# Seven block products in place of eight for 20 of the 22 column blocks of the first feed-forward matrix

## The reference, cut to what matters

```
def swiglu(x, w_in, w_out):
    a, b = jnp.split(x @ w_in, 2, axis=-1)
    return (jax.nn.silu(a) * b) @ w_out
...
        h = swiglu(x, w_ffn_in[l], w_ffn_out[l])
        x = layer_norm(ALPHA * x + h, ln3_g[l], ln3_b[l])
```

## Time and profile before

| | |
|---|---|
| median of 3 runs | 891.89 us (891.59 to 893.75) |
| the profiled execution's own time | 891.73 us |
| its span (first to last instruction) | 890.0 us |
| TensorE busy | 879.4 us, 99% |
| weight loads busy | 732.5 us, 82% |
| VectorE busy | 420.9 us, 47% |
| ScalarE busy | 292.3 us, 33% |
| GpSimd busy | 53.2 us, 6% |

### The profile page before, as it was taken

One profiled execution on the slowest core, in us unless ns is written; L12 is line 12 of the kernel. 1 busy time (PEld: TensorE's weight loads), 2 busy tenths in 40 slices (PEclk: granted clock), 3 DMA queues, 4 the chain that ended last, 5 costly groups with the idle time before them and its releaser, 6 DMA issues.

```text
span 890.0 us, 11559 instructions
## 1 busy us (share of the span) xinstructions
PE 879.4 (99%) x4519; PEld 732.5 (82%) x4519; DVE 420.9 (47%) x780; ACT 292.3 (33%) x544; POOL 53.2 (6%) x85
## 2 busy tenths in 40 slices
PE   8999999999999999999999999999999999999996
PEld 8988898877678888888889788888888888888885
DVE  4344357778533434434767693333333333322344
ACT  4112167238632222222325552222222222111221
POOL 3100000262300000000000010000000000000000
PEclk9999999999999999999999999999999999999999
DMA  8535532330013232326605111222222224323211
GB/s 283 161 95 141 119 96 60 107 95 2 1 49 94 95 95 94 94 94 236 220 18 189 48 49 48 94 94 94 94 94 94 94 94 142 105 102 105 104 81 71
DMA packets 70502, 90.11 MB, mean 101 GB/s; under 512 B 2861, under 2 KB 62071, under 8 KB 70463
## 3 DMA queue, kind: packets, MB, share of 16 engines
q1 hardware_dynamic: 70079, 89.15, 30.9%
q0 software_dynamic: 384, 0.43, 0.3%
HBM read 87.05 MB, written 2.52 MB: 101 GB/s over the span
## 4 chain that ended last, share of the span: by engine, by line
PE 96%; issue 1%; DVE 1%; DMA 1%; ACT 0%; SPq 0%; DVEq 0%; POOLq 0%; POOL 0%
PE ps L1738 28%; PE ps L1739 28%; PE ps L1740 28%; PE ps L1903 3%; PE ps L1980 2%; PE ps L1940 2%; PE ps L1775 1%; DMA x_nat<-in_x 1%; PE ps L2322 1%; PE ps L2323 1%; PE ps L2324 1%; PE ps L2252 0%; PE ps L1949 0%; PE ps L2255 0%; PE ps L2253 0%
## 5 line engine op out<-in xcount | busy, mean ns | idle before, releaser
L1738 PE MATMUL ps<-xt_hi,w_hi 128*128 128x512 f32 (+1 forms) x688 | 267.6, 389 | 0.2 <-DVE w_lo L1694 0.2
L1739 PE MATMUL ps<-xt_hi,w_lo 128*128 128x512 f32 (+1 forms) x688 | 266.8, 388 | 0.0
L1740 PE MATMUL ps<-xt_lo,w_hi 128*128 128x512 f32 (+1 forms) x688 | 266.8, 388 | 0.0
L1738 PEld LDWEIGHTS ps<-xt_hi,w_hi 128*128 128x128 f32 x688 | 129.2, 188 | 27.4 <-issue 0.6
L1740 PEld LDWEIGHTS ps<-xt_lo,w_hi 128*128 128x128 f32 x688 | 129.2, 188 | 26.4
L1739 PEld LDWEIGHTS ps<-xt_hi,w_lo 128*128 128x128 f32 x688 | 129.2, 188 | 26.3
L895 ACT CAST w_hi<-raw 128x1024 fp32r<-128x1024 f32 (+1 forms) x58 | 60.0, 1037 | 180.4 <-PE ps L1740 172.0
L1178 DVE TENSOR_TENSOR w_lo<-raw,w_hi 128x1024 fp32r<-128x1024 f32 (+1 forms) x58 | 70.1, 1210 | 91.1 <-ACT w_hi L895 90.7
L1694 DVE TENSOR_TENSOR w_lo<-raw,w_hi 128x1024 fp32r<-128x1024 f32 x40 | 48.9, 1222 | 79.1 <-ACT w_hi L1137 79.1
L1487 DVE TENSOR_TENSOR w_lo<-raw,w_hi 128x1024 fp32r<-128x1024 f32 x30 | 36.7, 1223 | 90.1 <-ACT w_hi L1062 90.1
L1137 ACT CAST w_hi<-raw 128x1024 fp32r<-128x1024 f32 x40 | 41.9, 1047 | 78.8 <-PE ps L1740 78.8
(11 more groups left out here) (288 smaller groups left out, 1293.8 us busy)
## 6 DMA issues: line engine op xcount, KB each, us to landing
raw<-in_w_in SPq DMA_DIRECT2D x24, 1024.0 KB, 5.0
raw<-in_w_ffn_in SPq DMA_DIRECT2D x22, 1024.0 KB, 4.9
raw<-in_w_ffn_out SPq DMA_DIRECT2D x11, 1024.0 KB, 4.8
raw<-in_w_mix_out SPq DMA_DIRECT2D x4, 1024.0 KB, 4.8
raw<-in_w_branch_b SPq DMA_DIRECT2D x4, 512.0 KB, 4.0
resid<-in_x SPq DMA_DIRECT2D x1, 2048.0 KB, 9.5
raw<-in_w_xkv SPq DMA_DIRECT2D x2, 1024.0 KB, 5.7
raw<-in_w_in SPq DMA_DIRECT2D x3, 512.0 KB, 4.1
```

The costliest lines, as they stand in the source:

```text
L1738: pe.matmul(dst, a_hi, b_hi, start=start, stop=False)
L1739: pe.matmul(dst, a_lo, b_hi, start=False, stop=False)
L1740: return pe.matmul(dst, a_hi, b_lo, start=False, stop=stop)
```

## The change

The first group of four pieces stays. The remaining 20 double pieces of 256 columns ("blocks", n = 0 to 19; even ones are of the silu half, odd ones of the other half, and a pair of them gives two slices of hidden activations) are each computed by Winograd's form of Strassen's scheme. Each block is seen as a product of 2 by 2 quarters: the 1024 summed columns in two halves, the 256 weight columns in two halves of 128, the 512 rows in two halves of 256. Seven products of quarters, P1 to P7, take the place of eight. Each product is 4 slices by 3 matmuls of 128 weight columns against 256 rows, 12 matmuls; a block is 84 matmuls of 256 rows where it was 48 of 512.

Four sums of quarters of the activations are made once (`SUM1` to `SUM4`; GpSimd makes two inputs and SUM3, VectorE the rest), and split like everything else (`sum_round` on ScalarE, `sum_rest` on VectorE). Four sums of quarters of the weights are made by VectorE for each block: `t1`, `t2`, `t3` (in place in `raw`) and `t4`. Each of the seven weight operands is split by ScalarE (`op_round`) and VectorE (`op_rest`) into one of four slots of half the old size. Three bank copies per block by ScalarE (`seed`, `hold_u2`, `hold_u3`) and two additions by VectorE (`add_c22`, `add_c12`) bring the products together. ScalarE instead of VectorE now rounds the hidden activations (`round_first`, `round_second`). SyncE loads each block as two halves of 512 KB; the loops are written out. In the first slice of the second matrix TensorE takes the four tiles of 128 rows in the order 0, 2, 1, 3 in place of 2, 3, 0, 1.

In the diff `pool` is GpSimd, `act` ScalarE, `dve` VectorE and `pe` TensorE; the first `ffn_block` is ScalarE's, the second VectorE's, and the loop after it VectorE's too. GpSimd calls `left_sums` ahead of the last norm's first `rstd`.

```
+def products_in_order():
+    order = []
+    for n in range(N_BLOCK):
+        order.append(("P1", n))
+        if n:
+            order.append(("P4", n - 1))
+        order.append(("P5", n))
+        if n:
+            order.append(("P3", n - 1))
+        order += [("P6", n), ("P2", n), ("P7", n)]
+    return order + [("P4", N_BLOCK - 1), ("P3", N_BLOCK - 1)]
...
+            def left_sums():
+                pool.wait_ge(turn_lo, 4 * TT + 4)
+                pool.tensor_tensor(F11, xt_hi[:, 0:4, LO].bitcast(F32), xt_lo[:, 0:4, LO].bitcast(F32), ALU.add).then_inc(left_sum, 1)
+                pool.tensor_tensor(F12, xt_hi[:, 4:8, LO].bitcast(F32), xt_lo[:, 4:8, LO].bitcast(F32), ALU.add).then_inc(left_sum, 1)
+                pool.wait_ge(left_sum, 1)
+                pool.wait_ge(right_sum, 1)
+                pool.tensor_tensor(SUM3, F11, F21, ALU.subtract).then_inc(sum3_done, 1)
...
+            def op_round(kind, n):
...
+                if m >= 4:
+                    act.wait_ge(prod_done, m - 3)
...
+                act.copy(op_slot(m, 0), right_operand(kind, n)).then_inc(op_hi, 1)
...
+            def hold_u3(n):
+                act.wait_ge(prod_done, PRODUCT["P7", n] + 1)
+                act.copy(held(n)[:, HI], bank_c(n)).then_inc(u3_done, 1)
+            def silu_left(n):
+                act.wait_ge(prod_done, PRODUCT["P2", n] + 1)
+                act.wait_ge(h_done, n + 1)
+                act.activation(sa[:, 0, LO], bank_a(n), ACT.Silu).then_inc(silu0_done, 1)
...
+            def ffn_block(n):
+                odd, j = n % 2, n // 2 - 1
+                if n:
+                    hold_u3(n - 1)
+                    op_round("P3", n - 1)
+                seed(n)
+                op_round("P6", n)
+                if odd:
+                    silu_right(n - 1)
+                op_round("P2", n)
+                op_round("P7", n)
+                if not odd and n:
+                    round_first(j)
+                hold_u2(n)
+                op_round("P1", n + 1)
+                if odd:
+                    silu_second(n - 1)
+                else:
+                    silu_left(n)
+                op_round("P4", n)
+                op_round("P5", n + 1)
+                if not odd and n:
+                    round_second(j)
...
+            def ffn_block(n):
...
+                if n:
+                    add_c22(n - 1)
+                    op_rest("P3", n - 1)
+                weight_t2(n)
+                op_rest("P6", n)
+                if not odd and n:
+                    times_right(j)
+                if odd and n > 1:
+                    hidden_rest(j, 1)
+                op_rest("P2", n)
+                op_rest("P7", n)
+                weight_t4(n)
+                if n:
+                    add_c12(n - 1)
+                op_rest("P1", n + 1)
+                if not odd and n:
+                    hidden_rest(j, 0)
+                    times_second(j)
+                op_rest("P4", n)
+                weight_sums(n + 1)
+                op_rest("P5", n + 1)
+                if odd:
+                    times_left(n // 2)
...
+            for n in range(N_BLOCK):
+                ffn_block(n)
+                if n == 0:
+                    first_hidden(1)
+                    sum_rest(3)
+                    sum_rest(4)
...
+            def product(kind, n):
+                m = PRODUCT[kind, n]
+                pe.wait_ge(op_lo, m + 1)
+                if n == 0 and kind in ("P5", "P6", "P7", "P3"):
+                    pe.wait_ge(sum_lo, {"P5": 1, "P6": 2, "P7": 3, "P3": 4}[kind])
...
+                elif kind == "P7":
+                    pe.wait_ge(u2_done, n + 1)
+                elif kind == "P4":
+                    pe.wait_ge(u3_done, n + 1)
```

More of the change, by code:

```diff
@@ L1139, in ffn_iteration @@
[L1139 to L1155, removed]
+            def first_silu(q):
+                act.wait_ge(piece_done, PF + q + 1)
+                act.activation(sa[:, q, :], ps[:, q, :], ACT.Silu).then_inc(silu_done, 1)
+            def sum_round(j):
+                if j == 3:
+                    act.wait_ge(sum3_done, 1)
+                else:
+                    act.wait_ge(sum_done, min(j, 3))
+                if j == 4:
+                    act.wait_ge(piece_done, PF + 4)
+                act.copy(x_sum(j, 0), (SUM1, SUM2, SUM3, SUM4)[j - 1]).then_inc(sum_hi, 1)
@@ new lines, in _ @@
+            first_silu(0)
+            sum_round(1)
+            first_silu(1)
+            sum_round(2)
+            op_round("P1", 0)
+            op_round("P5", 0)
+            sum_round(3)
+            for n in range(N_BLOCK):
+                ffn_block(n)
+                if n == 0:
+                    sum_round(4)
+            split(PO)
+            hold_u3(LAST)
+            op_round("P3", LAST)
+            split(PO + 1)
+            round_first(LAST // 2)
+            round_second(LAST // 2)
@@ L1156, in _ @@
+            for n in range(2, FF_T):
                 split(PO + n)
@@ L1697, in ffn_iteration @@
[L1697 to L1717, removed]
@@ L1724, in _ @@
+            add_c22(LAST)
+            op_rest("P3", LAST)
+            times_right(LAST // 2)
+            add_c12(LAST)
+            rest_of(PO + 1)
+            times_second(LAST // 2)
+            hidden_rest(LAST // 2, 0)
+            hidden_rest(LAST // 2, 1)
+            for n in range(2, FF_T):
                 rest_of(PO + n)
@@ L2298, in _ @@
+            for n in range(N_BLOCK):
+                product("P1", n)
+                if n:
+                    product("P4", n - 1)
+                product("P5", n)
+                if n:
+                    product("P3", n - 1)
+                product("P6", n)
+                product("P2", n)
+                product("P7", n)
+            product("P4", LAST)
+            product("P3", LAST)
             for k in range(FF_T - N_TAIL):
[L2299 removed]
+                pe.wait_ge(lo_done, counted(PO + k) + 1)
```

317 lines of the change are left out of this document (262 added, 55 removed).

## The result

The changed kernel takes 922.75 us (median, 922.05 to 923.75), the kernel before 891.77 beside it: a ratio of 1.034, with a 95% interval of 1.0325 to 1.0361. It is slower, as forecast, but by 31.0 us and not by 18. In the profiled executions the span grew from 890.0 to 920.3 us, by 30.3. All of that lies in the stage that was rewritten: the second matrix starts at 793.29, and in the kernel before at 763.00, also 30.3 us apart.

The account below looks back on a forecast made before the run. TensorE, busy 99%, was taken to set the time. Stage with its waits +11.8, GpSimd holding VectorE +4.7 and clock +1.5 made 18.0 on 891.73: 909.7, say 910 us, range 900 to 916.

Parts of the forecast that it names:

- What TensorE saves: Rewritten stage: 20 blocks of 84 matmuls at 0.120 us take 201.6 for 217.7, 16.1 us less if nothing waits.
- Even blocks: P4 of even blocks 2 to 18 waits 1.85 us for `hold_u3` in ScalarE's in-order queue, nine times, 16.7 us.
- The chain: Even blocks, from P6's result through ScalarE and VectorE to `hold_u3` and P4: 6.01 us, against 4.16 on TensorE.
- Odd blocks: P4 of odd blocks: 4.22 us until its bank copy against 4.16, a wait of 0.06, nine times, 0.5 us.
- The start: First products wait 8.3 us: 0.7 before P1(0), 0.8 before P6(0), 6.8 before P7(0) for `s3_lo`.
- GpSimd beside VectorE: At the start, GpSimd sums hold VectorE's last norm operation 2.4 us and SUM1 2.3: +4.7 us.
- The waits of 1.85 are shorter than 2.7, so no loss there.: Even blocks' recurring waits: the clock fell 2.7 us after the last work at the kernel's end, so 0 us lost.
- the clock does not hold at the recurring waits either: Rival: half speed for as long as each of the nine waits lasts, 9 x 0.9, 918 us; chance 7%.
- The clock at the start: Waits of 3 and 6.8 us at the start lower the clock: between nothing and 3.4 us lost, 1.5 taken.
- GpSimd is not free: Judges the rival that GpSimd does not hold VectorE at the start, other terms standing: 905 us; chance 27%.
- No half load was late: Judges the rival that half loads come 0.5 us late in each of 9 even blocks: +4.5, 914; chance 9%.
- VectorE's load binds: Sign of a wrong forecast: TensorE waits for `w_lo` of P5 or P6, so VectorE's load, not ScalarE's queue, is the bound.

Follow-up runs that it names:

- the kernel of 9: Changed kernel with ScalarE's and VectorE's queues rewritten for the whole stage, all sums on VectorE, arithmetic and TensorE's order kept: 882.61 us, ratio 0.9890.
- (2): Changed kernel with `round_second` moved behind `hold_u3` in ScalarE's queue: 907.46 us, ratio 1.0173.
- (3): Changed kernel with ScalarE's copy `hold_u3` moved ahead of the cast of P5 in every block but the first: 900.20 us, ratio 1.0092.
- (4): Kernel of (3) with GpSimd's three sums cut from 1024 columns to 16, their readers taking other sums of the same size: 896.28 us, ratio 1.0044.
- experiments 1: Changed kernel plus 14 unused 256-row matmuls on TensorE before P4 of each even block from 2 on: 912.90 us, ratio 1.0226.
- (7): Kernel of (3) plus 52 unused 256-column multiplications on TensorE in the wait before P7 of block 0: 897.48 us, ratio 1.0059.
- that of 5: Changed kernel with GpSimd's three sums (F11, F12, SUM3) made by VectorE instead: 923.39 us, ratio 1.0346.
- (6): Changed kernel with `sum_rest(3)`, the low half of P7(0)'s left factor, moved on VectorE ahead of block 1's weight sums: 918.37 us, ratio 1.0293.
- the two moves of 8: Changed kernel with `hold_u3` ahead of the cast of P5, block 0 included, and `sum_rest(3)` early as in (6): 894.48 us, ratio 1.0029.

## Why the prediction was right or wrong

- **What TensorE saves.** Right: steps of 0.12, 84 to a block, 16.1 us; the kernel of 9 cashes in what its waits leave of them.
- **Even blocks.** Right in place and cause: by moving one link of the chain (2) or the copy itself (3) the wait shrank and went. In size it cost 2.00 from start to start, nine times, for 1.85. The chain came out as written but for its last link: the copy `hold_u3` ends at 590.38 (590.02 and 0.36) and P4 starts at 590.53, a hand-over of 0.15 where 0.04 stood. That the row shows 1.84 is chance, since it counts from the modelled end of the matmul before.
- **Odd blocks.** Right in place; the distance there is 0.33 in place of 0.12, by the same hand-over (the copy ends at 578.24, P4 starts at 578.38). With a restart I had 0.16 for each and it was 0.28. Even and odd blocks together came out 2.2 us dearer, and the start 1.3 cheaper; these nearly cancel.
- **The start.** P7(0) waited 6.7 for 6.8, behind the operations named; P1(0) 2.8 and the residual 1.4, P6(0) 0.6. With the lock, 12.0 us for 13.3.
- **GpSimd beside VectorE.** Right: each engine held the other, in the two places that were named. Mis-sized a little: a turn cost VectorE 2.0 and 2.1, not 2.4 and 2.3, and 3.9 us of time (4), not 4.7. "SBUF — State Buffer" of the Trainium skill, section "SBUF: two separate sides", states both directions of the lock; the rows of 3.30 and 3.31 now show the one that no row of before had.
- **The clock. This step failed:** "The waits of 1.85 are shorter than 2.7, so no loss there." The 2.7 us were the stretch from the last matmul at the kernel's end to the fall, read as the least idle time that can lower the clock. That is one idle stretch after steady work, not a limit for idle stretches that come back. Seven of nine waits of 1.84 lowered it, 10.2 us in all (experiments 1 and 2). The rival "the clock does not hold at the recurring waits either" was the true case, and had its cost too low as well: half speed for as long as each wait makes 0.9; it was 1.5, since the clock falls after the wait, when TensorE works, and stays down for some 3 us. The Trainium skill, "TensorE: Matmul & The Clock Gate", section "A second HAM failure mode: psum-queue depth-cycling", tells of such short recurring idles at which the clock swings; I weighed that at 7% against one row of another kind, and the trace agrees with it (seven falls). That nine waits of 1.32 cost nothing in the clock, it doesn't tell.
- **The clock at the start.** 2.5 to 2.7 (7) for the 1.5 taken; the bound of 3.4 held.
- **The other rivals.** GpSimd is not free (rows, and 4). No half load was late: they land 4.3 us after their issue (median of the page) for 4.5 allowed, and one that was late would have made some of the nine waits longer than 1.84. VectorE's load binds only once the wait on ScalarE is gone (3).

What stays open: why the first two of the nine waits left the clock alone, and why the number of falls differs between kernels whose recurring waits are alike (seven in the changed kernel, eight in that of 5), and why the time that the clock is down differs between executions of one kernel (6).

## What to carry to other kernels

When a change cuts TensorE's work but brings waits that recur, price each wait twice: once as time, and once as a fall of the clock behind it, here 1.5 us for a wait of 1.84, unless a row of the same kind of wait shows that it holds. Before such a change is given up, write down the in-order queues of the engines that serve TensorE and look for the copy that frees a bank but stands behind a cast that waits; the two moves of 8 were worth 28 us here, and a full reordering turned 3.4% slower into 1.1% faster. And a row is evidence only for its own kind of event: one idle stretch at the end says nothing of nine in the middle.

## What the runs showed of the hardware that was not expected

- The granted clock fell to 0.50 after seven of nine waits of 1.84 us, 22.5 to 24 us apart, and after none of nine of 1.32 us. It fell only after work had begun again: the first slow distance comes 0.9 us after P4's start at 635.52 (0.76 in 636 to 637, back at 1.00 in 640 to 641) and 0.4 us after the one at 779.44.
- The same wait may or may not cost it: after the 2.8 us before P1 of block 0 the clock was 1.00 in the changed kernel, and in the kernels of experiments 1 and 8, where that part is unchanged, it was down (0.70 in 8; here 1):

```profile
550.00:555.00 5.00, 4.94 (x30) 0.71 0.00 2
```

- A GpSimd sum of 1024 columns takes about 2.25 us once it has its turn, worked out from the rows (535.49 less 533.25; and 2.26 for SUM3, 540.57 less 538.31, the end of VectorE's operation before it), and its row shows over 3 where it stood for VectorE first. Even with 16 columns the first was 0.89 long while VectorE's norm operation ran (529.29 to 530.18, VectorE until 530.11).
- TensorE started 0.15 us after the end of the ScalarE copy that it waited for (590.38 to 590.53), while VectorE starts 0.04 after the end of a ScalarE cast.
